# Expert weights with consecutive matrix lines in one partition, the other operands read with a step

## The reference

```python
def moe_tokens(xt, w_router, b_router, w_gate, w_up, w_down):
    ...  # gate: for each token the weight of its two experts, 0 for the other 14
    h = jax.nn.silu(jnp.einsum('nd,edf->nef', xt, w_gate)) * jnp.einsum('nd,edf->nef', xt, w_up)
    return jnp.einsum('nef,efd->nd', h * gate[:, :, None].astype(h.dtype), w_down)
```

## Time and profile before

| what | value |
|---|---|
| time, median of 3 runs | 1413.61 us (1412.34 to 1415.68) |
| span of the profiled execution, first to last instruction | 1410.6 us |
| TensorE busy (matmuls, PE) | 1271.5 us, 90% of the span |
| TensorE weight loads (PEld) | 774.7 us, 55% |
| VectorE, ScalarE, GpSimd busy | 598.6, 307.6, 239.2 us |
| TensorE's clock, mean granted | 0.923 of full |
| moved by DMA | 319.70 MB, mean 227 GB/s |

### The profile page before, as it was taken

How to read it: one execution, slowest core, us unless ns; L and a number is a source line. 1 busy time by engine, 2 the same in 40 slices (tenths; PEclk the granted TensorE clock), 3 DMA queues, 4 the chain that set the end, 5 groups by cost and what they waited for, 6 DMA issues and landing times.

```text
span 1410.6 us, 15211 instructions
## 1 busy us (share of the span) xinstructions
PE 1271.5 (90%) x5858; PEld 774.7 (55%) x5858; DVE 598.6 (42%) x1108; ACT 307.6 (22%) x506; POOL 239.2 (17%) x92
## 2 busy tenths in 40 slices
PE   4999999889799999999599999699798799999993
PEld 3877656554554455443478843267577644444441
DVE  3668566342411222222779357637623212222225
ACT  3244235120201111112234200343320111111111
POOL 5434300000000000000555501324370000000000
PEclk9889978999769999999799999899899599999997
DMA  8133270356619999988134489743327479999961
GB/s 275 63 120 123 108 279 13 119 185 210 232 44 367 379 381 381 379 331 298 33 120 136 163 288 395 275 145 119 120 87 294 185 268 384 383 381 381 349 237 38
DMA packets 132170, 319.70 MB, mean 227 GB/s; under 512 B 4674, under 2 KB 4706, under 8 KB 131986
## 3 DMA queue, kind: packets, MB, share of 16 engines
q1 hardware_dynamic: 123794, 288.93, 56.1%
q0 software_dynamic: 8032, 28.79, 5.6%
q10 hardware_dynamic: 288, 1.20, 0.2%
HBM read 296.02 MB, written 22.89 MB: 226 GB/s over the span
## 4 chain that ended last, share of the span: by engine, by line
PE 79%; DVE 13%; ACT 3%; issue 3%; DMA 1%; DVEq 0%; SPq 0%; POOL 0%; ACTq 0%; POOLq 0%
PE bank L1035 22%; PE bank L876 16%; PE bank L851 11%; PE bank L905 8%; PE bank L1279 4%; PE bank L1195 3%; DVE arena L2186 2%; PE bank L863 2%; PE bank L864 1%; PE bank L1131 1%; PE bank L1062 1%; PE bank L1158 1%; PE bank L1012 1%; DMA ring<-in_w_in_attn 1%; DVE arena L1808 1%
## 5 line engine op out<-in xcount | busy, mean ns | idle before, releaser
L615 POOL TENSOR_TENSOR ring_parts<-ring,ring_parts 128x4096 fp32r<-128x4096 f32 x22 | 198.0, 9004 | 460.3 <-ACT ring_parts L610 460.1
L1035 PE MATMUL bank<-ring_parts,XTt_parts 128*128 128x512 f32 (+1 forms) x624 | 203.8, 407 | 8.3 <-DVE ring_parts L1881 6.7
L1035 PE MATMUL bank<-ring_parts 128*128 128x512 f32 x616 | 197.8, 398 | 0.0
L876 PE MATMUL bank<-ring,XTt 128*64 128x512 f32 x768 | 171.8, 604 | 1.5 <-issue 1.5
L851 PE MATMUL bank<-arena,Xt 128*128 128x128 f32 (+1 forms) x768 | 149.5, 329 | 0.1
L1035 PEld LDWEIGHTS bank<-ring_parts,XTt_parts 128*128 128x128 f32 x624 | 121.0, 198 | 36.7 <-issue 10.4
L851 PEld LDWEIGHTS bank<-arena,Xt 128*128 128x128 f32 (+1 forms) x768 | 114.1, 204 | 43.7 <-issue 18.1
L1035 PEld LDWEIGHTS bank<-ring_parts 128*128 128x128 f32 x616 | 118.1, 193 | 26.0 <-issue 1.5
L876 PEld LDWEIGHTS bank<-ring,XTt 128*64 128x64 f32 x768 | 57.1, 140 | 112.6 <-issue 112.6
L905 PE MATMUL bank<-ring,XTt 128*64 128x512 f32 x512 | 113.4, 595 | 0.0
L610 ACT ACTIVATE ring_parts<-ring 128x4096 fp32r<-128x4096 f32 (+1 forms) x24 | 83.3, 3476 | 80.3 <-DMA ring<-in_w_in_ret 74.1
(11 more groups left out here) (255 smaller groups left out, 1398.8 us busy)
## 6 DMA issues: line engine op xcount, KB each, us to landing
ring<-in_w_exp_down SPq DMA_DIRECT2D x32, 2048.0 KB, 8.7
ring<-in_w_exp_up SPq DMA_DIRECT2D x32, 2048.0 KB, 15.6
ring<-in_w_exp_gate SPq DMA_DIRECT2D x16, 2048.0 KB, 11.8
arena<-in_w_exp_gate SPq DMA_DIRECT2D x16, 2048.0 KB, 16.1
ring<-in_w_in_ret SPq DMA_DIRECT2D x12, 2048.0 KB, 8.2
ring<-in_state_ret SPq DMA_DIRECT2D x8, 2048.0 KB, 14.4
out_state_s<-ring POOLq DMA_DIRECT2D x8, 2048.0 KB, 12.6
ring<-in_w_in_attn SPq DMA_DIRECT2D x7, 2048.0 KB, 9.0
```

Of the source, the lines that this page charges most:

```text
L615: pool.tensor_tensor(single(weights(key)), weights(key), rounded(key), ALU.subtract).then_inc(low_ready, 1)
L876: last = pe.matmul(ps[64 * j:64 * j + 64, :], xs[:, k, 64 * j:64 * j + 64], w[:, k, :], start=(k == 0), stop=(k == KC - 1))
L1035: last = pe.matmul(ps[:, 0:width], x(t, a, k), w[c][:, k, 0:width], **at)
```

## The change

Row `p * 8 + k` of a gate or up matrix now lies in partition `p`, block `k` (row `p * 4 + k` of a down matrix). A partition's part of a load is then one piece of 16 KB of memory, since 8 rows of 2 KB, or 4 of 4 KB, follow one another. The destination in SBUF has the same shape and place. So that the other operands fit, the gather for block `k` takes the token's numbers `k`, `k + 8`, `k + 16`, ...: a view `XK` of `X` with a step of 8 floats. And the turn for block `m` takes the numbers `m`, `m + 4`, ... of `hid`: a view `hidm` with a step of 4 floats. Both are operands that TensorE loads as weights. No instruction is added, removed or moved on any engine.

```diff
         X = Xt[:, :].rearrange("p (t d) -> p t d", t=3)
+        XK = Xt[:, :].rearrange("p (t q k) -> p t k q", t=3, k=KC)
...
+        hidm = hid.rearrange("p (q m) -> p m q", m=4)
...
         def expert_weights(L, what, e):
             w = (A["w_exp_gate"], A["w_exp_up"], A["w_exp_down"])[what]
-            return w[L, e].rearrange("(k p) n -> p k n", p=128)
+            return w[L, e].rearrange("(p k) n -> p k n", p=128)
...
-            src = w[L, bass.ds(p * 2 + j % 2, 1)].rearrange("o (k p) n -> p (o k) n", p=128)
+            src = w[L, bass.ds(p * 2 + j % 2, 1)].rearrange("o (p k) n -> p (o k) n", p=128)
...
-                            r, d = ROWS[t], slice((4 * h + c) * 128, (4 * h + c + 1) * 128)
-                            last = pe.matmul(ps[:, c * 128:(c + 1) * 128], X[0:r, t, d], OH[0:r, t].rearrange("p j s -> p (j s)"),
+                            r = ROWS[t]
+                            last = pe.matmul(ps[:, c * 128:(c + 1) * 128], XK[0:r, t, 4 * h + c, :], OH[0:r, t].rearrange("p j s -> p (j s)"),
                                              start=(t == 0), stop=(t == 2))
...
-                    last = pe.transpose(ps[:, m * 128:(m + 1) * 128], hid[:, m * 128:(m + 1) * 128], ident)
+                    last = pe.transpose(ps[:, m * 128:(m + 1) * 128], hidm[:, m, :], ident)
```

More of the change, by code:

```diff
@@ L678, in body @@
                 for name, buf in (("gate", 0), ("up", 1), ("down", 0)):
-                    src = A["w_exp_" + name][L, bass.ds(e, 1)].rearrange("o (k p) n -> p (o k) n", p=128)
+                    src = A["w_exp_" + name][L, bass.ds(e, 1)].rearrange("o (p k) n -> p (o k) n", p=128)
                     sp.wait_ge(S["pe"], n * OV["pe"] + (3 if name == "down" else 1))
@@ L929, in over_body @@
                         r = ROWS[t]
-                        last = pe.matmul(bank[0][:, c * 64:(c + 1) * 64], X[0:r, t, c * 128:(c + 1) * 128], OH[0:r, t, 0, :],
+                        last = pe.matmul(bank[0][:, c * 64:(c + 1) * 64], XK[0:r, t, c, :], OH[0:r, t, 0, :],
                                          start=(t == 0), stop=(t == 2))
@@ L941, in over_body @@
                 for m in range(4):
-                    last = pe.transpose(bank[4][:, m * 128:(m + 1) * 128], hid[:, m * 128:(m + 1) * 128], ident)
+                    last = pe.transpose(bank[4][:, m * 128:(m + 1) * 128], hidm[:, m, :], ident)
                 last.then_inc(S["pe"], 1)
```

## The result

The changed kernel takes 1538.8 us (1538.53 to 1540.54), the kernel before 1412.97 on the same chip: a ratio of 1.089, 95% interval 1.0874 to 1.0905, 126 us slower. The forecast had the direction and the place, but the time lies beyond its 1519. Further down, one of six executions of the kernel with rows dealt in twos took 2464.71 us, and nothing on record says why; its ratio leaves that one out.

A forecast was written before the change was run, and what follows sets the result against it. TensorE was taken to bound both expert stages. Later gathers 66, first gathers 8, turn 4 and transfers 0 made 78 us, added to 1413.6 for 1492 us; range 1411 to 1519, the forecast's own 1464 to 1519.

The forecast's parts named there:

- What bounds the kernel: Both expert stages: TensorE sets the pace at 33.2 us a pair of experts; weight transfers follow narrowly, DMA engines 95.9% busy.
- Transfers at 0: Expert weight loads: longer pieces may cut a pair's transfers to 29.9 us, hidden behind TensorE's 33.2, so worth 0.
- The stepped load: Gather's TensorE loads of X with a step of 8 floats: +98 ns each, 672 loads, 66 us (49 to 83).
- VectorE's two readings: Step price carried from VectorE sums to a gather load: by ratio +73 ns, by time per element +123; middle taken.
- at or over the edge already: Gather: at 176 ns per load and matmul, between 107 and 211, any load time beyond 107 lies on the path.
- The clock: Later gathers and pairs: granted clock stays at 1.00 despite slower loads, no term in the sum; forecast's chance 0.57.
- rival 3: Later gathers: the stretched gather loses the clock, some 9 us more per pair, 126 us, about 1552 us; chance 0.06.
- First gathers: First gather of each stage, at half clock: stepped loads cost 1 to 14 us, middle 8.
- The turn: Turn of hid, loads with a step of 4 floats: between hidden and 8 us, middle 4.
- 1 (the step is free): Gather's loads: the step costs 0 ns, so the time stays 1413.6 us, give or take 2; chance 0.27.
- 2: Expert pairs: shorter transfers relieve something unseen on TensorE, 5 us faster, 1408 us; chance 0.07.
- 4: Expert weight transfers: longer pieces move slower, at 300 GB/s 42 us a pair, 122 us more, 1536; chance 0.03.

The follow-up runs named there:

- the run of the loads alone: Changed kernel with X and hid read contiguously, weights still in 16 KB pieces, against the kernel before: 1413.71 us, ratio 0.9997.

## Why the prediction was wrong

**What bounds the kernel**: right. TensorE kept the pace in both kernels, and faster transfers alone gave a ratio of 0.9997.

**Transfers at 0**: right for this change, and for the reason given. The 45 us named as most at stake, were TensorE's cover gone, were not tested: with TensorE down to 30.45 us a pair, 16 KB pieces gave 14.

**The stepped load**: the mechanism was right, its size too small. The sum had +98 ns a load; the path shows (14.5 - 8.45)/48 = 126 ns, and the load itself grew by 146 ns at full clock, to 334, above the 260 to 315 that would have shown the forecast right. Of VectorE's two readings the time per element (+123) came close to the path and the ratio (+73) did not; the middle was no reading at all. That VectorE and TensorE share a reason no run shows, so the closeness may be luck. The reading that loads were "at or over the edge already" was wrong: in a row they were hidden (0.11 us each), and the mean of 176 ns came from the steps between 128 and 64 rows. What followed from it, that a longer load lies on the path, held all the same. 14 gathers by 6.05 us are 85 us, where the sum had 66. With that alone, and the two small terms below, the time would have been about 1503, within the forecast's own range.

**The clock**: this is the step that failed. The forecast was "loads with a step slower, clock stays", and its sum has nothing for the clock. A falling clock stood as rival 3 with 0.06, as another way in which things could go; it happened together with the forecast, in every one of the 14 gathers. Six pairs of the changed kernel take 41.8 us each from gate to gate, 8.6 more than before: 6.05 by the loads, 0.1 by the turn (3.95 to 4.07 us in the run with the turn's step alone), and the rest, 2.5 us, by the clock: 1.3 in the gather (15.8 - 14.5) and 1.2 in turn and scatter. 14 by 2.5 us are 35 us. Rival 3 had 9 us more per pair, near the 8.6, but by other parts: 6.6 for the gather (7.3 measured) and 2.6 for a slow gate, where the clock was back and the products took 13.83 us as before; what slowed was turn and scatter. The warning stood in the prediction's own: the gather alone, at 0.50, did not lift the clock. Why a stretch of longer loads, with TensorE never idle in it, loses the clock stays open; the runs show that it does with the step in the gather, and not with the new transfers or the turn's step alone.

**First gathers**: 16.27 us instead of the 15.06 before, 2.4 us for both; the sum had 8.

**The turn**: 4 in the sum, about 2 measured. Whether a step of 16 bytes costs as much as one of 32 was told by the gather (329 and 334 ns at full clock), not by the turn.

The sum again with measured terms: 85 + 35 + 2 + 2 = 124, for 126 us. The first pair of each stage lost a little more than the others (9.2 and 11.2 us), its down products running in part at half clock.

**The rivals**: 1 (the step is free) holds for 2 floats only, nearly; 2 and 4 fell with the run of the loads alone (0.9997).

## What to carry to other kernels

A layout that makes transfers better and an engine's reads worse is judged by which of them sets the pace; here the faster transfers were hidden and the slower loads were not. Keep two neighbouring floats together in whatever TensorE loads as weights: dealing the rows in twos kept the reads cheap and still doubled the pieces. When a stretch of TensorE's work is made sparser, ask for the clock as part of the forecast, not as a rival to it, and look for switches between loads of different row counts, which here cost 43 us where larger pieces gained 14 at most.

## What was not expected of the hardware

- A load of 128 columns with a step of 4 to 16 floats takes 309 to 334 ns (medians) at either clock; a contiguous one 188 at full and 332 at half clock. At half clock the step is nearly free: the first gather lost 1.2 us of 15.
- Going from loads of 128 rows to loads of 64 and back cost some 0.2 us each time in the gather; without 12 of 16 such switches it took 6.14 instead of 8.45 us, and the kernel 43 us less (some 12 of them in the two first gathers).
- In the changed kernel the clock fell 3.5 to 5.8 us after each of the 14 later gathers began, with TensorE busy throughout; with the same loads in blocks of 1.8 us between dense products it was 1.00 in one stage and 0.98 in the other.
